# A fused three-layer network on one core: a reordered opening, reworked heads, and counted multiplications of constants ahead of TensorE's long waits

## What is computed

```python
cond = jax.nn.silu(c)
for layer in range(2):
    sh1, sc1, g1, sh2, sc2, g2 = split(cond @ ada_w[layer] + ada_b[layer], 6)
    h = modulate(rmsnorm(x, norm_g[layer, 0]), sh1, sc1)      # h * (1 + scale) + shift
    mixed = ssd_na_mixer(h, ...) if layer == 0 else mlstm_mixer(h, ...)
    x = x + g1 * rmsnorm(mixed, norm_g[layer, 1])
    h = modulate(rmsnorm(x, norm_g[layer, 2]), sh2, sc2)
    u = square(relu(h @ mlp_w1[layer])) @ mlp_w2[layer]
    x = x + g2 * rmsnorm(u, norm_g[layer, 3])
# second block, one layer
proj = rmsnorm(x, norm_mix) @ w_in                            # split for three branches and gates
merged = gate0 * (fox @ wb0) + gate1 * (s5 @ wb1) + gate2 * (hgrn2 @ wb2)
x = x + merged @ w_out
x = x + cross_attention(rmsnorm(x, norm_x), rmsnorm(mem, norm_mem), xq, xk, xv, xo, ...)
x = x + swiglu(rmsnorm(x, norm_ffn), w_gate_up, w_down)
```

## Time and profile before

| what | us |
|---|---|
| median of three runs | 1724.01 (1722.21 to 1725.61) |
| the profiled execution, its own time | 1722.36 |
| its span in the trace | 1720.5 |
| PE busy | 1573.7 (91%) |
| VectorE busy | 1163.7 (68%) |
| ScalarE busy | 791.8 (46%) |
| GpSimd busy | 59.4 (3%) |
| mean granted clock of PE | 0.957 |
| DMA | 292.83 MB, 170 GB/s in the mean |

### The profile page before, as it was taken

One profiled execution on the slowest core, in us unless ns is written; L12 is line 12 of the kernel. 1 busy time (PEld: TensorE's weight loads), 2 busy tenths in 40 slices (PEclk: granted clock), 3 DMA queues, 4 the chain that ended last, 5 costly groups with the idle time before them and its releaser, 6 DMA issues.

```text
span 1720.5 us, 22558 instructions
## 1 busy us (share of the span) xinstructions
PE 1573.7 (91%) x8999; PEld 1331.3 (77%) x9002; DVE 1163.7 (68%) x1813; ACT 791.8 (46%) x1069; POOL 59.4 (3%) x72
## 2 busy tenths in 40 slices
PE   5878997998999979999989997999988998899998
PEld 4678885567998877887789986866775677789997
DVE  6779776546877586676677575899873485556653
ACT  4443555444553343644454532756533554344342
POOL 0000000000000000000000002440010000000000
PEclk8988998998999989999989998999998999999999
DMA  9865552322766746343536553322332343235551
GB/s 363 327 244 213 206 221 74 124 85 102 268 243 224 289 150 248 141 147 122 197 144 250 182 187 143 123 98 97 124 123 74 125 158 136 89 138 189 175 193 74
DMA packets 41223, 292.83 MB, mean 170 GB/s; under 512 B 4512, under 2 KB 4640, under 8 KB 6560
## 3 DMA queue, kind: packets, MB, share of 16 engines
q1 hardware_dynamic: 39968, 284.04, 44.7%
q10 hardware_dynamic: 1152, 7.34, 1.1%
HBM read 288.22 MB, written 3.15 MB: 169 GB/s over the span
## 4 chain that ended last, share of the span: by engine, by line
PE 69%; DVE 17%; ACT 5%; issue 3%; POOL 1%; ACTq 0%; DVEq 0%; POOLq 0%
PE ps L980 30%; PE ps L988 26%; DVE ring_at_lo L1159 4%; ACT w_hi L1148 2%; DVE arena_at L1078 2%; PE ps L2391 1%; DVE arena_at L1971 1%; PE ps L3057 1%; PE ps L2849 1%; PE ps L1846 1%; PE ps L2149 1%; PE ps L947 1%; PE ps L2123 1%; PE ps L2133 1%; PE ps L2836 1%
## 5 line engine op out<-in xcount | busy, mean ns | idle before, releaser
L1159 DVE TENSOR_TENSOR ring_at_lo<-ring_at,w_hi 128x2048 fp32r<-128x2048 f32 (+1 forms) x218 | 495.6, 2274 | 221.5 <-ACT w_hi L1148 221.5
L1148 ACT ACTIVATE w_hi<-ring_at 128x2048 fp32r<-128x2048 f32 (+1 forms) x218 | 415.7, 1907 | 255.5 <-PE ps L980 153.8
L988 PE MATMUL ps<-h_hi,w_hi 128*128 128x256 f32 x1440 | 419.7, 291 | 12.0 <-DVE hT_at_lo L1429 6.4
L988 PE MATMUL ps<-h_hi,ring_at_lo 128*128 128x256 f32 x1440 | 419.7, 291 | 0.0
L988 PE MATMUL ps<-hT_at_lo,w_hi 128*128 128x256 f32 x1440 | 415.2, 288 | 0.0
L980 PE MATMUL ps<-w_hi,arena_at_lo 128*128 128x512 f32 x1232 | 395.1, 402 | 7.7 <-DVE arena_at_lo L743 4.0
L988 PEld LDWEIGHTS ps<-h_hi,w_hi 128*128 128x128 f32 x1440 | 283.3, 197 | 22.1 <-issue 17.7
L980 PEld LDWEIGHTS ps<-w_hi,arena_at_lo 128*128 128x128 f32 x1232 | 232.9, 192 | 65.4 <-issue 10.5
L988 PEld LDWEIGHTS ps<-h_hi,ring_at_lo 128*128 128x128 f32 x1440 | 281.6, 196 | 0.0
L988 PEld LDWEIGHTS ps<-hT_at_lo,w_hi 128*128 128x128 f32 x1440 | 279.5, 194 | 0.3
L980 PE MATMUL ps<-ring_at_lo,arena_at_lo 128*128 128x512 f32 x616 | 245.9, 399 | 0.0
(11 more groups left out here) (457 smaller groups left out, 1662.8 us busy)
## 6 DMA issues: line engine op xcount, KB each, us to landing
ring_at<-stream SPq DMA_DIRECT2D x266, 1024.0 KB, 4.8
arena_at<-bias ACTq DMA_DIRECT2D x4, 768.0 KB, 5.8
kept<-arena_at ACTq DMA_DIRECT2D x2, 1024.0 KB, 5.2
arena_at<-kept ACTq DMA_DIRECT2D x2, 1024.0 KB, 7.5
arena_at<-mem SPq DMA_DIRECT2D x1, 1024.0 KB, 6.5
x_res<-x SPq DMA_DIRECT2D x1, 1024.0 KB, 16.4
out<-x_res SPq DMA_DIRECT2D x2, 512.0 KB, 2.8
par<-params SPq DMA_DIRECT2D x1, 698.0 KB, 4.2
```

The lines of the kernel that those rows point to most:

```text
L988: mm = pe.matmul(k.ps[:, bank + q // 2, (q % 2) * TOK:(q % 2 + 1) * TOK], w[:, q * P:(q + 1) * P], x, start=first and n == 0 and q % 2 == ...
L1148: act.activation(k.w_hi[:, s % HI, 0:n, :], k.ring[:, c % RING, 0:n, :], ACT.Identity).then_inc(k.hi_done, 1)
L1159: dve.tensor_tensor(k.w_lo[:, c % RING, 0:n, :], k.ring[:, c % RING, 0:n, :], k.w_hi[:, s % HI, 0:n, :].bitcast(F32), ALU.subtract).then_i ...
```

## The change

It has three parts.

**The opening.** The parameters come in two transfers; the first 200 columns (102 KB) are sent first, then the early constants, chunk 0, mem, chunks 1 to 4, x, chunks 5 and 6, and then the other 1196 columns of the parameters. Guests in mem stand behind own chunks 1, 3, 5, 7 (before: 1, 2, 4, 5), and the first four groups are ordered as shift and scale of the first half of the channels, then of the second. FirstNorm is made in two halves, each as soon as its guests are taken. mem and in0 are one `Chain` in one `Woven`, with no `meet` between them; BiasLoad is a lead of in0. The tables of SSD and of the norm are shifted by the 32 quarters of mem.

**The heads.** `rstd_pair` takes the place of sum, mean and rstd; the division by 1024 goes into the squares as a scale of 1/32, and each round works on the two columns one after the other (L506, L510), waiting for all but the last operation issued. The gain row is laid out by PE in Join itself, and ScalarE takes it behind the squares.

**Counted multiplications.** `keep_busy(pe, k, bank, n)` issues n products of the identity with ones, 128x128 with 128x256 in float32, into a bank whose content nobody needs. There are 271 calls' worth: 9 ahead of mem, 11, 7, 21, 6, 3 and 9 ahead of six of the guests' columns, 11 in SSD, 31 at the neighbours' first turn, 7, 4, 18 and 25 at the end of out0, down0, out1 and down1, 4 (where there is a gain row), 6 (2 at up1) and 7 in each head, 7 in HGRN, 20 in Fox, 5 and 5 at merged, 9 at norm_x, 7 in the cross attention.

The diff, cut to its core:

```diff
-GUESTS = {"mem": [1, 2, 4, 5], "in0": [2, 4, 6, 8, 10, 12, 14, 16], "up0": [3, 7, 11], "down0": [3, 7, 11], "in1": [1, 3, 5],
+GUESTS = {"mem": [1, 3, 5, 7], "in0": [2, 4, 6, 8, 10, 12, 14, 16], "up0": [3, 7, 11], "down0": [3, 7, 11], "in1": [1, 3, 5],
           "out1": [3], "up1": [3, 9]}
-GUEST_GROUPS = ada_groups(0, 0, 6) + ada_groups(1, 0, 6)
+GUEST_FILL = {0: 11, 1: 7, 4: 21, 6: 6, 18: 3, 19: 9}
+FIRST_PARTS = [(0, 0), (1, 0), (0, 1), (1, 1)]
+GUEST_GROUPS = [ada_groups(0, part, part + 1)[half] for part, half in FIRST_PARTS] + ada_groups(0, 2, 6) + \
+    ada_groups(1, 0, 6)
...
+def rstd_pair(dve, st, a, b, var, half, y, tmp, done):
+
+
+
+    st(dve.scalar_tensor_tensor(var, a, EPS, b, ALU.add, ALU.add))
+    st.wait()
+    st(dve.tensor_scalar(y.bitcast(I32), var.bitcast(I32), -0.5, float(0x5f3759df), ALU.mult, ALU.add))
+    st(dve.tensor_scalar(half, var, -0.5, None, ALU.mult))
+    st.wait()
+    for n in range(3):
+        for t in range(TT):
+            at = slice(t, t + 1)
+            if n:
+                st.wait_before(1)
+            st(dve.scalar_tensor_tensor(tmp[:, at], y[:, at], y[:, at], half[:, at], ALU.mult, ALU.mult))
+        for t in range(TT):
+            at = slice(t, t + 1)
+            st.wait_before(1)
+            last = dve.scalar_tensor_tensor(y[:, at], tmp[:, at], 1.5, y[:, at], ALU.add, ALU.mult)
+            if n < 2:
+                st(last)
+            else:
+                last.then_inc(done.sem, 1)
+                if t == 0:
+                    st.wait()
...
+def keep_busy(pe, k, bank, n):
+
+    for _ in range(n):
+        pe.matmul(k.ps[:, bank, 0:TOK], k.con("ident"), k.con("ones"), start=True, stop=True)
...
+        for half in range(2):
+            act.wait_ge(k.guest_took, 2 * half + 2)
+            for f in range(4 * half, 4 * half + 4):
+                act.wait_ge(*m["bank_turned"].at(f // 2 + 1))
+                src = k.ps[:, self.bank(f), (f % 2) * TOK:(f % 2 + 1) * TOK]
+                st(act.activation(k.hT[:, f, :], src, ACT.Identity, scale=self.scale[:, f:f + 1],
+                                  bias=self.shift[:, f:f + 1]))
                 st.wait()
-                ins.then_inc(m["turned_hi"].sem, 1)
-        yield
+                act.activation(k.h_hi[:, f, :], src, ACT.Identity, scale=self.scale[:, f:f + 1],
+                               bias=self.shift[:, f:f + 1]).then_inc(m["turned_hi"].sem, 1)
+            yield
+            if half == 0:
+                yield
...
     def turn_pair(self, pe, j):
-        for wait in [*self.ready(j), *self.freed]:
+        for wait in self.freed:
+            pe.wait_ge(*wait)
+        keep_busy(pe, self.k, 4 + j, self.fill.get(j, 0))
+        for wait in self.ready(j):
...
         for n, c in self.guests_after.get(e, []):
-            pe.wait_ge(*k.guest_step(n, KD))
             if n >= 1:
                 pe.wait_ge(k.guest_took, n)
+            keep_busy(pe, k, ADA, GUEST_FILL.get(n, 0))
+            pe.wait_ge(*k.guest_step(n, KD))
             for q in range(4):
...
+    def tensor(self, pe):
+        yield from super().tensor(pe)
+        k, n = self.k, self.first_group + 1
+        pe.wait_ge(k.act_took, k.act_groups[n])
+        pe.wait_ge(k.dve_took, k.dve_groups[n])
+        keep_busy(pe, k, self.pair(0), self.fill)
...
+        if self.gain is not None:
+            self.gain.lay_out(pe)
+            keep_busy(pe, k, 4, 4)
...
-        for wait in [*self.post.taken(), *self.freed]:
+        for wait in self.post.taken():
             pe.wait_ge(*wait)
-        pe.wait_ge(*m["rate_in"].at(1))
+        keep_busy(pe, k, self.bank, 2 if self.gain is None and self.shift is not None else 6)
+        pe.wait_ge(*m["rate_in"].at(2))
         for t in range(TT):
             mm = pe.matmul(k.ps[:, self.bank, t * P:(t + 1) * P],
                            self.post.small[:, 16 + t:17 + t].broadcast_to([P, P]), k.con("ident"), start=True, stop=True)
         mm.then_inc(m["rate_laid_out"].sem, 1)
+        keep_busy(pe, k, self.bank + 1, 7)
...
-        st(dve.tensor_tensor(s[:, 4:6], s[:, 0:2], s[:, 2:4], ALU.add))
-        st.wait()
-        st(dve.tensor_scalar(s[:, 4:6], s[:, 4:6], 1.0 / D, EPS, ALU.mult, ALU.add))
-        rstd(dve, st, s[:, 4:6], s[:, 6:8], s[:, 8:10], m["post_rate_in"])
-        dve.wait_ge(*m["post_rate_in"].at(1))
+        rstd_pair(dve, st, s[:, 0:2], s[:, 2:4], s[:, 4:6], s[:, 20:22], s[:, 6:8], s[:, 8:10], m["post_rate_in"])
+        dve.wait_ge(*m["post_rate_in"].at(2))
...
+        keep_busy(pe, k, 4, 11)
         pe.wait_ge(*m["silu_in"].at(1))
...
+            if h == 0:
+                keep_busy(pe, k, 6, 31)
             pe.wait_ge(*m["shares_in"].at(h + 1))
...
+    out1 = PostProduct(k, "out1", cell, y, junk2, small, guest, 18)
...
+            if i == 4:
+                keep_busy(pe, k, 4, 7)
             pe.wait_ge(*m["ops"].at(i + 1))
...
+        pe.wait_ge(*self.hgrn.m["copied"].at(2))
+        keep_busy(pe, k, 4, 20)
         pe.wait_ge(*m["qk_scaled"].at(TT))
-        pe.wait_ge(*self.hgrn.m["copied"].at(2))
...
+                pe.wait_ge(*m["probs_in"].at(1))
+                keep_busy(pe, k, 4, 7)
                 pe.wait_ge(*m["probs_taken"].at(2))
...
-                        [key_norm.m["key_in"].at(4)])
+                        [key_norm.m["key_in"].at(4)], [(0, 5), (2, 5)])
...
+    out0 = PostProduct(k, "out0", src, y, junk, small, fill=7)
...
-        Woven(k, mem, (Threaded(mem_rates), paced([(0, 2, 2, 6)])), (Threaded(first_norm), paced([(0, 3, 8, 20), (3, 6, 24, 27), (6, 7, 28, 29)], True)),
-              (Threaded(keep), paced([(0, 1, 17, 18)], True))),
-        BiasLoad(na),
-        Woven(k, in0, (Threaded(ssd), ssd_due), (Threaded(norm), norm_due), (tail, na_in)),
+        Woven(k, Chain(k, mem, in0), (Threaded(mem_rates), paced([(0, 2, 2, 6)])),
+              (Threaded(first_norm), paced([(0, 3, 8, 17), (3, 4, 19, 20), (4, 5, 21, 22), (5, 6, 27, 28), (6, 7, 32, 33)])),
+              (Threaded(keep), paced([(0, 1, 17, 18), (1, 2, 33, 36)])),
+              (Threaded(ssd), ssd_due), (Threaded(norm), norm_due), (tail, na_in)),
...
+    down = PostProduct(k, f"down{layer}", Operand(None, uo.hi, uo.lo, hidden.made), y, junk, small, guest, 4 if layer == 0 else 25)
...
-            sp.dma_start(k.par_all[:, :], params).then_inc(k.params_in, 16)
+            first = k.where_p["conv_w"][0]
+            sp.dma_start(k.par_all[:, 0:first], params[:, 0:first]).then_inc(k.params_in, 16)
 
             def load(c, slot):
                 sp.dma_start(k.ring[:, slot, :, :], stream[c]).then_inc(k.loaded[slot], 16)
 
             early = k.where_c["levels"][0]
             sp.dma_start(k.con_all[:, 0:early], consts[:, 0:early]).then_inc(k.ident_in, 16)
+            load(0, 0)
             sp.dma_start(mem_rows, mem[0].rearrange("(t p) d -> p t d", p=P)).then_inc(k.mem_in, 16)
-            for c in range(RING):
+            for c in range(1, RING):
                 load(c, c)
-                if c == 3:
+                if c == 4:
                     sp.dma_start(k.x[:, :, :], x[0].rearrange("(t p) d -> p t d", p=P)).then_inc(k.x_in, 16)
+            sp.dma_start(k.par_all[:, first:], params[:, first:]).then_inc(k.inputs_in, 16)
             sp.dma_start(k.con_all[:, early:], consts[:, early:]).then_inc(k.inputs_in, 16)
...
```

158 lines of the change are left out of this document (78 added, 80 removed).

## The result

The changed kernel takes 1728.64 us (median of 20 runs, 1725.07 to 1733.69) against 1722.58 (1716.28 to 1727.40) for the kernel before in the same sessions: a ratio of 1.0035, 95% interval 1.0025 to 1.0045. The forecast was no difference that can be measured, 1723; it is about 6 us slower, more than the 3.4 us that I had set as the bound.

What follows compares the result with a forecast made beforehand. TensorE ended the longest chain of waits for 69%, VectorE for 17%; time was lost in PE's waits and half-clock windows. The terms -13 + 2.3 + 16.6 - 7.3 + 0.8 = -0.6 on 1723.4 gave 1723 us, range 1710 to 1738.

Steps and rivals of the forecast that it cites:

- Fills ahead of a barrier: Ends of out0, down0, out1, down1: fills ahead of `meet` hold back ScalarE and VectorE too, +16.6 us.
- Opening: Mem to in0: earlier chunk 0, no barrier, norm in halves and a warmer clock save time, -13 us.
- rival A: Slower: VectorE's in-order queue bounds the opening, which gives little more than the first product's gain, -5; 1731 us; chance 0.20.
- Neighbours: Neighbours' first turn: 31 calls outlast the wait, +4.3, full clock behind gives -2.0; net +2.3 us.
- Heads: Four heads (Join): paired rstd, gain row and squares -6.3, fills' overshoot +5.0, full clock -6.0; net -7.3 us.
- Second block: HGRN 0, Fox +0.3, merged -1.5, norm_x -1.0, cross attention +3.0; together +0.8 us.
- Cross attention's 3.0: Cross attention: its 7 calls stand behind the wait that ended the idle time, so they add all 3.0 us.
- B: Slower: the fills don't hold the clock, so the clock gains go and half-clock calls take twice as long; 1735 us; chance 0.10.
- C: Slower: the rstd pair gains nothing, its 15 operations taking 2.95 us a chain; 1733 us; chance 0.05.
- D: Faster: the opening gives its bound of 20 us, since late chunks, not VectorE, end the guests' waits; 1716 us; chance 0.18.
- E: Faster: fills ahead of the barrier cost no more than a few us; 1707 us; chance 0.07.
- The rule on transposes: Heads: if PE transposes aren't activity, fills lift the clock and -6.0 us is whole; otherwise it could shrink to -3.

Runs made afterwards that it cites:

- experiment 9: Changed kernel with only the 7, 4, 18 and 25 calls ahead of the four barriers, all other fills zero: 1725.38 us, ratio 1.0027.
- experiment 1: Changed kernel without the 7, 4, 18 and 25 calls ahead of the four barriers, all else kept: 1713.15 us, ratio 0.9950.
- experiment 2: Changed kernel with keep_busy doing nothing, so no fill anywhere: 1709.64 us, ratio 0.9932 to the kernel before.
- experiment 5: Kernel without any fill plus the opening's fills alone (9, 11, 7, 21, 6 and SSD's 11): 1712.66 us, ratio 0.9954.
- Experiment 10: Kernel with only fills that fit their waits (1702.62 us), with 31 calls in place of 20 at the neighbours' first turn: 1707.12 us, ratio 0.9914.
- experiment 11: Kernel without any fill plus merged's first 5 calls and the cross attention's 7, both behind their wait: 1715.64 us, ratio 0.9960.
- experiment 7: Kernel without any fill, with the old rstd chain on both columns at once in the four heads, scaled squares kept: 1713.59 us, ratio 0.9954.
- experiment 6: Kernel without any fill, with the neighbourhood tables' two transfers issued 17 quarters of chunks later: 1710.04 us, ratio 0.9937.
- experiment 13: Kernel without any fill, with 1.6 MB of late parameters, constants and masks issued behind chunk 10 of the stream: 1712.09 us, ratio 0.9949.

## Why the prediction was wrong, point by point

- **Fills ahead of a barrier, +16.6:** right, and in its mechanism. Alone they cost 15.7 (experiment 9), taken out they give back 15 (experiment 1), and the starts of VectorE's rstd are at 8.0 and 11.0 us behind PE's last product where 7.8 and 10.8 were forecast.
- **Opening, -13:** this is the step that failed; it measured -5.3. The first product's -3.6 was -3.2. From there to in0's first product -8.3 was forecast and -4.3 came; behind it -2, and +2.2 came. These two terms were added up from the barrier, the features and the clock, as if what PE saves there were saved in the end. The chain of the changed kernel runs elsewhere: a transfer for 13.0 us, ScalarE and VectorE for 27.8, and in in0 a transfer of 12.3. The landings were in the trace of before and never laid against the forecast: by its 10 us windows transfers moved 418 GB/s from 10 to 30 us. Chunks 14 to 19 land only 0.1 to 1.9 us earlier in the changed kernel, and 20 to 22, beside the tables, 4.7 to 8.1 later. Without fills the opening holds 8.5 (experiment 2). Its own fills take 3 (experiment 5), a price that I had put at +1 for the 21 calls and at nothing for the others; and it comes through the chunk of in0, not through the length of the 21. The time came out where rival A had put it, -5. Its cause, VectorE's queue, has a part in it, as the chain shows; how large a part no run tells, since none changes VectorE's order alone.
- **Neighbours, +2.3:** the fill added 4.4, as worked out, and the clock behind it gave back some 3, so the piece is +1.3. Experiment 10 shows 11 calls of its length alone: 4.5 by the medians, 4.6 in the traces.
- **Heads, -7.3:** with the barrier terms the four heads were to give +9.3 and gave +9.6 in the ledger. Inside, the chain is 1.96 and not 1.73 us, -0.40 in place of -0.63, and with the gain row and the order of the squares the heads without fills are 4.1 us shorter where 6.3 was forecast. The overshoot of the fills was 3.2 and not 5.0, the clock at the first 24 products gave 5.1 against before where 6.0 was put. That makes -6.0, too little by 1.3; that the four heads' sum fits to 0.3 is in part luck.
- **Second block, +0.8:** +2.5, of it +1.1 ahead of and in Fox where +0.3 was put. Cross attention's 3.0 was seen, its sign and its cause; that merged's first fill stands behind its wait in the same way was overlooked (the wait on `freed` was taken for an idle one), and the two cost 6.0 by the medians and 2.5 in the trace (experiment 11) where 3.0 - 1.5 had been put.
- **Rivals:** B is out: 12 of 28 stretches are left, and the 24 products behind each head run at full clock where fills stand right ahead of them. C is out by experiment 7, whose chain of 2.17 us the pair does in 1.96. D is out, the opening gave 5.3 and not 20, and E, the fills ahead of the barrier cost 15.7.
- **The rule on transposes** (that they don't count as activity) from the Trainium skill, "TensorE: Matmul & The Clock Gate", Part 4, isn't decided here, but a second trace speaks against it too: in experiment 2, without any fill, the granted clock is 0.50 from 851.8 us and back at 1.0 from 855.2, and from 846.8 on PE had done nothing but transposes, the first at 851.96.

In the sum, the opening was put 7.7 us too good and the second block 1.7, heads 0.3, the neighbours 1.0 too bad: 8.7 us, from -0.6 to the ledger's +8.1.

## What to carry to other kernels

Filling a wait of TensorE paid here only where the fill stands ahead of the semaphore that ends the idle time, is not much longer than that wait at its own measured rate, and has no drain or barrier between it and that wait; count it from a row of the same shape, and look in the new trace for idle time in the fill's own bracket, or still behind it. A high granted clock and a busy TensorE are no evidence of a gain. A fill also pays where it is a little longer than its wait, if the products right behind it then run at full clock: in the heads it cost 3.2 us and gave back 6.6 over the next 24 products, in single executions. Before an earlier start is credited in a streaming kernel, write the landing time of each transfer and the other engines' queues beside the schedule, and ask of each saved microsecond whether it is on the chain: here a saving on PE met a transfer of 13.0 us and 27.8 us of ScalarE and VectorE.

## What the runs showed that I had not expected

- Taking the wait for a chunk from 2.00 to 0.51 us changed nothing (experiment 6), since a wait on another engine grew from 4.52 to 6.01. Moving 1.6 MB of transfers by four chunks cost 2.5 us (experiment 13).
- A chunk of 1 MB that lands in 4.9 us alone took 12.3 us with a chunk of 1 MB issued 0.4 us ahead of it and 2.5 MB of other transfers beside it.
- The fill of 21 calls ends where the columns start, and still isn't what they wait for (experiment 5): a fill hides the wait behind it, so its place in the row of PE proves nothing.
- The pair's round of two steps on two columns takes 0.46 us, as in 860.85 to 861.31 of the changed kernel, not twice 0.196: the second column's operation starts 0.12 to 0.14 behind the first's, not 0.08, and the first column's next one only behind that.
